# A token gather split by columns around the first expert pair, and one combine matmul ahead of every second turn

## What is computed

```python
top_v, top_i = lax.top_k(e_logits, TOPK_EXPERT)          # 2 of the 8 experts of the token's group
w_top = jax.nn.softmax(top_v, axis=-1) * p_group[:, None]
comb = jnp.sum(jax.nn.one_hot(eid, N_EXPERTS, dtype=jnp.float32) * w_top[..., None], axis=1)
hg = jnp.einsum('nd,edf->nef', t, w_gate)                # 1024 -> 256, per expert
hu = jnp.einsum('nd,edf->nef', t, w_up)
a = jax.nn.silu(hg) * hu * comb[:, :, None].astype(h.dtype)
y = jnp.einsum('nef,efd->nd', a, w_down)                 # 256 -> 1024, per expert
```

## Time and profile before

| | |
|---|---|
| Median of 3 runs | 807.11 us (807.05 to 810.26) |
| The profiled execution's own time | 810.11 us |
| Its span on the core | 808.2 us |
| PE, DVE, ACT busy | 760.6, 346.9, 190.1 us |
| Mean traffic | 244 GB/s over the span, near 416 GB/s between 230 and 440 us |

### The profile page before, as it was taken

The page is one execution under the profiler, slowest core; times in us unless marked ns, Lnnn a source line. Parts: engine busy times, 40 slices in busy tenths (PEclk is TensorE's granted clock), DMA queues, the critical chain, the costliest instruction groups (busy, mean ns, idle before and its releaser), DMA issues.

```text
span 808.2 us, 9616 instructions
## 1 busy us (share of the span) xinstructions
PE 760.6 (94%) x3873; PEld 503.8 (62%) x3873; DVE 346.9 (43%) x734; ACT 190.1 (24%) x418; POOL 56.0 (7%) x56
## 2 busy tenths in 40 slices
PE   5799999899999999999989999999989999999986
PEld 3478778677434343433334885888878888884432
DVE  1136424654622121212121866255456565568235
ACT  5122333542411110111011346122212111111002
POOL 2142553000000000000001000000000000000000
PEclk9899999999999999999999999998999999999999
DMA  9977895635959999999999943311435636435101
GB/s 355 392 219 248 323 356 179 222 140 218 380 195 416 414 420 411 418 415 414 419 406 363 374 158 105 105 41 65 127 123 168 197 121 202 166 146 192 68 27 55
DMA packets 76632, 197.25 MB, mean 244 GB/s; under 512 B 3263, under 2 KB 37416, under 8 KB 70184
## 3 DMA queue, kind: packets, MB, share of 16 engines
q1 hardware_dynamic: 75632, 195.37, 64.4%
q10 hardware_dynamic: 664, 0.80, 0.3%
q0 software_dynamic: 288, 0.41, 0.2%
HBM read 195.33 MB, written 1.05 MB: 243 GB/s over the span
## 4 chain that ended last, share of the span: by engine, by line
PE 77%; SPq 8%; DVE 7%; DMA 5%; ACT 2%; issue 1%; DVEq 0%; ACTq 0%
PE ps L1451 16%; PE ps L1173 9%; PE ps L740 8%; PE ps L1512 8%; PE ps L863 6%; PE ps L1247 4%; SPq L556 4%; PE ps L1087 4%; DMA ring<-in_w_in 3%; DMA arena<-in_w_up 2%; SPq L562 2%; PE ps L872 2%; PE ps L1049 2%; PE ps L1256 2%; PE ps L1059 2%; PE ps L1157 2%
## 5 line engine op out<-in xcount | busy, mean ns | idle before, releaser
L1173 PE MATMUL ps<-ring,arena 128*64 128x512 f32 x352 | 77.5, 593 | 2.0 <-DMA ring<-in_w_up 1.8
L863 PE MATMUL ps<-hs,ring 128*128 128x256 f32 (+1 forms) x288 | 67.8, 391 | 1.9 <-DMA ring<-in_w_in 1.9
L863 PEld LDWEIGHTS ps<-hs,ring 128*128 128x128 f32 (+1 forms) x288 | 53.5, 190 | 13.8 <-issue 6.5
L1173 PEld LDWEIGHTS ps<-ring,arena 128*64 128x64 f32 x352 | 25.9, 137 | 52.2 <-issue 51.9
L2746 DVE SCALAR_TENSOR_TENSOR arena<-arena,own_rows,ps 128x256 f32<-128x256 f32 x16 | 7.7, 480 | 111.0 <-ACT arena L1833 111.0
L740 PE MATMUL ps<-hs,ring 128*128 128x256 f32 x240 | 53.1, 380 | 0.3 <-PE ps L740 0.3
L740 PEld LDWEIGHTS ps<-hs,ring 128*128 128x128 f32 x240 | 45.3, 190 | 6.9 <-issue 0.7
L1451 PE MATMUL ps<-arena,mixT 128*128 128x256 f32 x176 | 42.5, 385 | 3.5 <-DVE mixT L2632 3.5
L1451 PE MATMUL ps<-ring,mixT 128*128 128x256 f32 x176 | 42.6, 385 | 0.0
L1451 PE MATMUL ps<-ring,hs 128*128 128x256 f32 x176 | 41.7, 379 | 0.9 <-DVE xT L2620 0.9
L1247 PE MATMUL ps<-ring,arena 128*64 128x512 f32 x176 | 40.2, 598 | 1.1 <-issue 0.5
(11 more groups left out here) (468 smaller groups left out, 1238.9 us busy)
## 6 DMA issues: line engine op xcount, KB each, us to landing
ring<-in_w_down SPq DMA_DIRECT2D x23, 1024.0 KB, 19.1
ring<-in_w_gate_up SPq DMA_DIRECT2D x22, 1024.0 KB, 7.5
ring<-in_w_gate SPq DMA_DIRECT2D x20, 1024.0 KB, 16.3
ring<-in_w_up SPq DMA_DIRECT2D x20, 1024.0 KB, 17.5
ring<-in_w_ada SPq DMA_DIRECT2D x5, 3072.0 KB, 14.2
ring<-in_w_down SPq DMA_DIRECT2D x5, 2048.0 KB, 8.0
ring<-in_w_in SPq DMA_DIRECT2D x9, 1024.0 KB, 18.2
ring<-in_w_ada SPq DMA_DIRECT2D x16, 512.0 KB, 11.7
```

The source lines that it names most:

```text
L863: last = pe.matmul(o[0:n, 0:L], lhsT=w[:, k, lo:lo + n], rhs=hT[:, k, :], start=k == 0, stop=k == KT - 1)
L1173: last = pe.matmul(ps[WIN * h:WIN * (h + 1), 0, :].rearrange("p (g n) -> p g n", g=2), lhsT=xw[:, u, k, :], rhs=expert_gate_up(2 * n + h, ...
```

## The change

The gather no longer makes all 512 columns of all tiles ahead of team 0. `gather_first` makes the first 128 columns (`FIRST_COLS`, the windows of teams 0 and 1) of all eight tiles into banks 6 and 7. `gather_rest` makes the other 384 columns: of tiles 0 and 1 ahead of team 0's `gate_up`, of tiles 2 to 7 behind it, in the banks of `REST_BANK`. VectorE adds the shift to team 0's window straight from PSUM to `xw` (two instructions of 128 x 256), then to `xsT`. `clear_banks` moves behind team 0's `down_joined`. Expert 5's near quarters are loaded behind the gate and up weights of experts 6 and 7, after the whole gather. On every odd team after team 1 one tile of `combine_joined` moves ahead of the wait for the product.

```diff
@@ SyncE
-            sp.wait_ge(gather_done, 1)
-            load_quarter(5, 0, 0)
-            sp.wait_ge(gather_done, 1 + KT)
-            load_quarter(5, 1, 0)
             for team in range(HOMES // 2, TEAMS):
                 sp.wait_ge(gate_up_used, team - HOMES // 2 + 1)
...
+                if team == HOMES // 2:
+                    sp.wait_ge(gather_done, 1 + KT)
+                    for g in range(2):
+                        load_quarter(5, g, 0)
                 sp.wait_ge(chunk_used, 2 * (team - HOMES // 2) + 2)
@@ TensorE
+            def gather_first():
+                pe.wait_ge(htr_taken_a, 4)
+                for b in range(BLK):
+                    pe.wait_ge(pick_ready, b + 1)
+                    for j in range(KT):
+                        last = pe.matmul(ps[:, 6 + j // 4, (j % 4) * FIRST_COLS:(j % 4 + 1) * FIRST_COLS],
+                                         lhsT=tok[:, b, j * P:(j + 1) * P], rhs=pick[:, b, 0:FIRST_COLS],
+                                         start=b == 0 and j % 4 == 0, stop=b == BLK - 1, skip_group_check=True)
+                last.then_inc(gather_done, 1)
+            def gather_rest(tiles):
+                for j in tiles:
+                    if j == 6:
+                        pe.wait_ge(gather_taken_v, 4)
+                    if j == 3:
+                        pe.wait_ge(gather_taken_a, 1)
+                    for b in range(BLK):
+                        last = pe.matmul(ps[:, REST_BANK[j], 0:PAIRS - FIRST_COLS], lhsT=tok[:, b, j * P:(j + 1) * P],
+                                         rhs=pick[:, b, FIRST_COLS:PAIRS], start=b == 0, stop=b == BLK - 1)
+                    last.then_inc(gather_done, 1)
...
                 if u:
                     turn_puts(m)
+                    if n > 1:
+                        combine_joined(m - 1, JOINED[5:6])
...
-                    combine_joined(m - 1, JOINED[5:8] if u else JOINED[3:5])
+                    combine_joined(m - 1, JOINED[6:8] if u else JOINED[3:5])
...
-                gather()
+                gather_first()
+                gather_rest((0, 1))
                 weights_there(0)
                 gate_up(0, 0, first=True).then_inc(gu_done, 1)
-                clear_banks()
+                gather_rest(range(2, KT))
                 pe.wait_ge(act_ready, 2)
+                pe.wait_ge(gather_taken_a, 2)
                 turn_act(0)
                 pe.wait_ge(turn_taken, 1)
+                pe.wait_ge(gather_taken_v, 6)
                 down_joined(0)
+                clear_banks(8)
@@ VectorE
-                take_gathered((1, 3, 5))
-                copy_window(0, starts[0], slice(0, FIRST_TILES)).then_inc(first_windows, 1)
-                take_gathered((7,))
-                copy_window(0, starts[0], slice(FIRST_TILES, KT)).then_inc(first_windows, 1)
+                ve.wait_ge(gather_done, 1)
+                for n, (bank, to) in enumerate(((0, xw[:, 0, :, :]), (1, xw[:, 0, :, :]), (0, xsT[:, :, 0:FIRST_COLS]),
+                                                (1, xsT[:, :, 0:FIRST_COLS]))):
...
+                    ve.tensor_tensor(to[:, tiles], first, shift_q[:, tiles].unsqueeze(2).broadcast_to([P, 4, cols_n]),
+                                     ALU.add).then_inc(first_windows if n < 2 else gather_taken_v, 1 if n < 2 else 2)
+                take_rest(1)
```

More of the change, by code:

```diff
@@ L108 @@
 GROUP_COLS = 8
-FIRST_TILES = 6
+FIRST_COLS = 2 * WIN
+REST_BANK = (2, 3, 1, 2, 4, 5, 6, 7)
 ROUTE_COLS = GROUP_COLS + EXPERTS
@@ L1162, in gather @@
                         last.then_inc(gather_done, 1)
+            def gather_first():
[17 more added lines that the diff above has]
+                    last.then_inc(gather_done, 1)
             def gate_up(n, u, first=False, late=False):
                 for k in range(KT):
-                    if first and k in (0, FIRST_TILES):
+                    if first and k in (0, KT // 2):
                         pe.wait_ge(first_windows, 1 if k == 0 else 2)
@@ L1206, in combine, with clear_banks @@
                 return last
-            def clear_banks():
+            def clear_banks(taken):
                 pe.wait_ge(gather_taken_a, 4)
-                pe.wait_ge(gather_taken_v, 4)
+                pe.wait_ge(gather_taken_v, taken)
                 for j in range(4):
@@ L1584, in _ @@
                 gather()
-                clear_banks()
+                clear_banks(4)
                 for team in range(TEAMS):
@@ L1825, in take_gathered, with take_rest @@
                                    ).then_inc(gather_taken_a, 1)
+            def take_rest(j):
+                act.wait_ge(gather_done, j + 2)
+                act.activation(xsT[:, j, FIRST_COLS:PAIRS], ps[:, REST_BANK[j], 0:PAIRS - FIRST_COLS], ACT.Identity,
+                               bias=shift_q[:, j:j + 1]).then_inc(gather_taken_a, 1)
             def team_act(n, u, fast):
@@ L1833, in team_act @@
                 act.activation(act_g, ps[:, 0, 0:FE], ACT.Silu).then_inc(silu_done, 1)
+                if fast and n == 0:
+                    for j in (2, 4, 6):
+                        take_rest(j)
                 act.wait_ge(turn_done, n + 1)
@@ L2007, in _ @@
             with act.If(too_many < 1):
-                take_gathered()
+                take_rest(0)
                 for n in range(TEAMS):
@@ L2422, in take_gathered, with take_rest @@
                 ve.wait_ge(gather_taken_a, (tiles[-1] + 1) // 2)
+            def take_rest(j):
+                ve.wait_ge(gather_done, j + 2)
+                ve.tensor_scalar(xsT[:, j, FIRST_COLS:PAIRS], ps[:, REST_BANK[j], 0:PAIRS - FIRST_COLS], shift_q[:, j:j + 1],
+                                 None, ALU.add).then_inc(gather_taken_v, 1)
             fast_steps = 2 * (TEAMS - 1)
@@ L2739, in _ @@
                 ve.sem_inc(windows_copied, 1)
-                take_gathered((1, 3, 5))
-                copy_window(0, starts[0], slice(0, FIRST_TILES)).then_inc(first_windows, 1)
-                take_gathered((7,))
-                copy_window(0, starts[0], slice(FIRST_TILES, KT)).then_inc(first_windows, 1)
+                ve.wait_ge(gather_done, 1)
+                for n, (bank, to) in enumerate(((0, xw[:, 0, :, :]), (1, xw[:, 0, :, :]), (0, xsT[:, :, 0:FIRST_COLS]),
+                                                (1, xsT[:, :, 0:FIRST_COLS]))):
+                    tiles, cols_n = slice(4 * bank, 4 * bank + 4), to.shape[-1]
+                    first = ps[:, 6 + bank, :].rearrange("p (k n) -> p k n", n=FIRST_COLS)[:, :, 0:cols_n]
+                    ve.tensor_tensor(to[:, tiles], first, shift_q[:, tiles].unsqueeze(2).broadcast_to([P, 4, cols_n]),
+                                     ALU.add).then_inc(first_windows if n < 2 else gather_taken_v, 1 if n < 2 else 2)
+                take_rest(1)
                 for n in range(TEAMS):
@@ L2750, in _ @@
                             starts = load(n + 1, 2)
+                        if n == 0:
+                            ve.wait_ge(gather_taken_v, 4)
+                        if n == 1:
+                            ve.wait_ge(gather_taken_v, 8)
+                            ve.wait_ge(gather_taken_a, 4)
                         copy_window((n + 1) % 2, starts[(n + 1) % 2])
                         put_rows_joined(n + 1).then_inc(windows_copied, 1)
+                    if n == 0:
+                        for j in (3, 5, 7):
+                            take_rest(j)
                     ve.wait_ge(chunk_used, 2 * n + 2)
```

## The result

Over 20 runs each, the changed kernel takes 811.66 us (809.3 to 818.04) and the kernel before 809.03 (806.78 to 816.72). The ratio is 1.0038, with an interval of 1.0019 to 1.0056: about 3.1 us slower (1.5 to 4.5). The medians alone differ by 2.6 us. Against the longer series the 807.11 shown of before was a low draw. The traced execution of the changed kernel spans 810.7 us.

The account below looks back on a forecast made before the run. The experts' weight stream, unbroken for 200 us, was taken to bound the kernel through when it gets going. Stream -0.1 and clock +1.3 gave +1.2 us on the 807.1 median: 808.3 us, range 803.6 to 811.6.

Parts of the forecast that it names:

- VectorE is late: Ahead of team 0: VectorE arrives at 220.1, TensorE starts at 220.75, 5.0 us sooner, after 2.9 us of new idleness.
- the sum: Whole kernel: stream -0.1 and clock +1.3 give +1.2 us, 808.3 on the median of 807.1.
- Team 1 later by 2.4: After the rest of the gather and the bare `clear_banks`, team 1 starts at 240.9 instead of 238.46.
- The stream level with before: Weight stream at team 4's first load: lands at 254.0 against 254.1, after a dry gap and second start; -0.1 us.
- lateness that costs nothing: Expert 5's two late quarters land by 242.6; team 2 needs them at 253.5, so their lateness costs nothing.
- The combine tile off the bounding chain: Seven odd teams save 0.43 us each, 3.0 in all, 2.15 before team 12; no gain in the end.
- the waits at teams 13 and 14 persist: Sign near the end of the experts' part: TensorE still waits for DMA weights at teams 13 and 14.
- The clock: TensorE at team 0: the 2.9 us idle time brings a half-speed stretch of 3.4 us, costing 1.3 us.
- rival B: Stream and teams as summed, but TensorE's clock holds after team 0's wait: 807.0 us; chance 0.25.

Follow-up runs that it names:

- all waits filled: Changed kernel plus three overwritten matmuls ahead of team 0 and two each ahead of teams 13 and 14; ratio 0.9991 to the kernel before.

## Why the prediction was right in the stream and wrong in the clock

The time forecast was 808.3 with a range up to 811.6; it came out at 811.66. The ratio was to be 1.0015 and is 1.0038. Point by point:

- **VectorE is late.** Right. I took its arrival 8.3 us after the gather's start; it was 219.34 - 210.98 = 8.4. Team 0 was to start at 8.9 and did. The flag's read took 0.5 us, the read of the two starts 1.1, and the rest with the branch 0.5, together 2.1; the sum had 2.1 for them. By the floor of about 0.6 us for a register load that the Trainium skill gives ("DMA: Bandwidth & Descriptors", section "Latency and other measured facts"), two loads would be 1.2 us and team 0's start 0.9 sooner. In the trace the two loads took 1.65, more than the two floors, and the branch comes on top.
- **Team 1 later by 2.4.** It was 2.6 (29.3 against 26.7). Gate and up with the rest of the gather took 15.0 us instead of 14.6, turn and copy 0.7 instead of 0.9.
- **The stream level with before.** Right in the main: 5 us sooner at the first load, a dry gap, a second start of 4.7 us, and a loss beside an instruction packet anew at 268.5. At team 13, where TensorE waits for the stream, it was 0.5 later (186.4 against 185.9 from the gather's start), and with the clock held G was 232.2, inside the 231.9 to 232.4 of before. The load order alone cost 3.2 us, so "lateness that costs nothing" was right for team 2 and the volume in the stream was the price, as the sum had it. One reading was loose: the slices of 406 to 420 GB/s run from 242 to 424 us, not from 232 to 440. Nothing in the sum hangs on it.
- **The combine tile off the bounding chain.** Right on the gain: 0.43 us saved on odd teams, none of it in the end. But the sum put the tile at nothing and asked no further, and this is **the step that failed**. Saving 0.43 on team 13 makes the wait at team 14 longer by as much, from 1.75 to 2.16; the tile alone, on the kernel before, gave the same 2.16. I had written that the waits at teams 13 and 14 persist and that 1.8 costs nothing, and never asked what 2.2 would cost. In the changed kernel the clock fell behind it in 3 of 4 traces, at 1.6 us each: 1.2 us on average where the sum had 0. The link from tile to time is less firm than that from tile to wait: the tile alone lost nothing on time, and behind 2.13 to 2.16 us in four other kernels the clock held.
- **The clock.** The second step that failed. The clock was to fall behind team 0's new wait, +1.3. In six traces with that wait at 2.53 to 2.56 us it never did: the term measured 0, and rival B had this place right. That the traces' loss of 1.35 us looks like the sum's +1.2 is luck, for the sum had the fall at a place where there was none and left it out where it came.
- **The base.** I set the sum on a median of three runs, 807.11; twenty gave 809.03. Of the 3.4 us between forecast and result 1.9 are this.

That falls of the clock make a good part of the timed loss, the timed executions show too. Over 32 of the changed kernel the mean granted clock is 0.9808, against 0.9835 over 97 of the kernel before: lower by 0.0027 (0.0013 to 0.0041), or 1.3 more stretches of 3.4 us at half clock in each. Among the 97, executions with 0.001 less clock took 0.66 us longer, so I estimate that 1.8 us of the loss go with the clock. With all waits filled the mean is 0.9841, and without the moved tile 0.9834.

What stays open is where the rest of it lies. The traces put 0.75 falls an execution and 1.35 us behind team 14; the timed runs lost 3.1 us (1.5 to 4.5) and, again, 0.43% (0.17 to 0.69). The further falls may be those ahead of the gather, where the traces of the changed kernel start it 2.3 us later on average, with a spread of 9 us. Whether the change brings these about, or chance did in four traces, no run here shows.

## What to carry to other kernels

Ask of a saving that ends in a wait how long the wait becomes: in these traces TensorE's waits for weights of up to 1.97 us were free, while one of 2.01 and three of eight of 2.10 to 2.16 us had half the clock behind them. When a stream of loads bounds, find what restarts it and what volume lies in it: an earlier start is lost again if the stream runs dry behind it and if loads move in from idle time. And before splitting work on one engine to start a second one sooner, look whether the engine between them is free by then; moving two additions ahead of VectorE's other work took 2.3 us off G, where the split itself, with the clock held, took off nothing.

## What the runs showed of the hardware

- A wait of one length gave both outcomes: behind 2.10 to 2.16 us at team 14 the clock fell in 3 of the 4 traces of the changed kernel, and in none of four other kernels with 2.13 to 2.16; behind 2.53 to 2.56 at team 0 in none of six; behind 2.01 at team 12 and behind 3.12 at team 14 in the one case seen of each. A wait's length alone does not decide.
- Where a 16 KB instruction packet ran in a stream that had just started from rest, landings came 1.3 to 1.4 us late: at 237.6 to 241.5 in the kernel before, at 264.8 to 268.5 in the changed one. Most later packets in a running stream cost nothing that the landings show, but in two traces a load landed 1.3 and 1.6 us late beside one. That the packets cause it is inferred from the times alone.
- Traced executions of one and the same kernel took 354.3 to 359.6 us from the second block to the end of TensorE's last matmul, and 211.0 to 219.8 us up to the gather. Each is more than the whole effect that was studied, and it is why ratios here rest on many runs.
